# Layer 0 in three parts: the sample first, tile 0's mixer beside its gathers, then tile 1

## The reference, cut to what matters

```python
for l in range(2):
    h = rmsnorm(x, norm_mix[l])
    out = mixer_ab(h, ...) if l == 0 else mixer_c(h, k_past, v_past, ...)
    x = x + out
    x = x + peer(rmsnorm(x, norm_ffn[l]), w_query[l], sub_keys[l], u[l], v[l])

def peer(x, ...):                                # 8 heads, 128 x 128 keys, 16 experts each
    qry = (x @ w_query).reshape(t, 8, 2, 128)
    sc = einsum('thpd,pnd->thpn', qry, sub_keys)
    idx, top = top 16 of all sums s1[i] + s2[j], from the top 16 of each half
    act = gelu(einsum('thed,td->the', u[idx], x))
    return einsum('the,thed->td', softmax(top) * act, v[idx])
```

## Time and profile before

| | |
|---|---|
| median of 3 runs | 1945.54 us (1941.55 to 1947.11) |
| the profiled execution | 1943.43 us, span 1941.7 us |
| busy: TensorE, VectorE, ScalarE, GpSimd | 62%, 63%, 37%, 37% of the span |
| moved by DMA | 720.74 MB, mean 371 GB/s |
| gathers (queue of GpSimd) | 604.02 MB; all else by SyncE 113.84 MB |
| mean granted clock of TensorE | 0.738 of full speed |

### The profile page before, as it was taken

One profiled execution on the slowest core, in us unless ns is written; L12 is line 12 of the kernel. 1 busy time (PEld: TensorE's weight loads), 2 busy tenths in 40 slices (PEclk: granted clock), 3 DMA queues, 4 the chain that ended last, 5 costly groups with the idle time before them and its releaser, 6 DMA issues.

```text
span 1941.7 us, 25073 instructions
## 1 busy us (share of the span) xinstructions
PE 1212.1 (62%) x9288; PEld 739.9 (38%) x9288; DVE 1225.5 (63%) x3079; ACT 723.0 (37%) x1937; POOL 726.5 (37%) x651
## 2 busy tenths in 40 slices
PE   7998865566667539855579546665666644444443
PEld 7896742233335307733248224443325400000000
DVE  4541558888755575476654674557865667677664
ACT  2322145534432335274333333237533334333322
POOL 2021024545433433333133444434533444454442
PEclk9999875676788859966689658778679955555555
DMA  5645389999999999999599999999999999999996
GB/s 192 205 142 162 126 319 397 421 388 421 420 418 418 419 421 393 417 418 393 205 373 416 420 421 417 418 419 414 375 420 418 420 421 422 422 420 422 421 421 273
DMA packets 115658, 720.74 MB, mean 371 GB/s; under 512 B 13424, under 2 KB 13552, under 8 KB 41296
## 3 DMA queue, kind: packets, MB, share of 16 engines
q0 software_dynamic: 82944, 604.02, 75.6%
q1 hardware_dynamic: 31584, 113.84, 15.9%
q10 hardware_dynamic: 1008, 1.29, 0.2%
HBM read 714.98 MB, written 4.12 MB: 370 GB/s over the span
## 4 chain that ended last, share of the span: by engine, by line
DMA 46%; PE 27%; DVE 15%; ACT 6%; issue 4%; POOL 2%; ACTq 0%; POOLq 0%; DVEq 0%; SPq 0%
DMA sb_AR<-in_uv,sb_idx 44%; PE PS L1429 10%; DVE sb_AR L1011 7%; PE PS L1674 5%; PE PS L1651 2%; PE PS L1571 2%; PE PS L1694 1%; POOL sb_AR L513 1%; DMA sb_W<-in_w 1%; ACT sb_DG L576 1%; DVE sb_AR L1063 1%; ACT sb_gl L573 1%; PE PS L1815 1%; ACT L573 1%; DMA sb_lq<-in_lq 1%
## 5 line engine op out<-in xcount | busy, mean ns | idle before, releaser
L513 POOL DMA_INDIRECT sb_AR<-in_uv,sb_idx x576 | 695.2, 1207 | 1042.1 <-PE PS L1674 910.4
L1011 DVE CUSTOM_DVE_ANT_0 sb_AR<-sb_AR 128x1024 f32<-128x1024 f32 x576 | 703.9, 1222 | 452.3 <-DMA sb_AR<-in_uv,sb_idx 447.6
L1674 PE MATMUL PS<-sb_AR,sb_DG 128*32 128x256 f32 x4608 | 509.7, 528 | 582.2 <-ACT sb_DG L576 559.6
L1674 PEld LDWEIGHTS PS<-sb_AR,sb_DG 128*32 128x32 f32 x4608 | 128.9, 129 | 893.7 <-ACT sb_DG L576 802.1
L573 ACT ACTIVATE sb_gl<-sb_dots 128x1 f32<-128x1 f32 x576 | 116.2, 202 | 875.5 <-DVE sb_dots L1011 874.2
L1429 PE MATMUL PS<-sb_hT,sb_W 128*128 128x160 f32 (+1 forms) x2304 | 345.8, 310 | 8.6 <-ACT sb_hT L547 3.3
L1429 PEld LDWEIGHTS PS<-sb_hT,sb_W 128*128 128x128 f32 x2304 | 322.8, 208 | 50.6 <-issue 24.8
L576 ACT ACTIVATE sb_DG<-sb_GR,sb_gl 128x32 f32<-128x32 f32 x576 | 185.1, 321 | 18.7
L573 ACT ACT_TABLE_LOAD x68 | 87.2, 1283 | 1.1
L558 ACT ACTIVATE sb_AR<-sb_Hn 32x1024 f32<-32x1024 f32 x72 | 75.8, 1053 | 1.5
L1651 PE MATMUL PS<-sb_W,sb_mixT 128*128 128x512 f32 x128 | 69.8, 672 | 6.0 <-DMA sb_W<-in_w 4.8
(11 more groups left out here) (357 smaller groups left out, 1193.3 us busy)
## 6 DMA issues: line engine op xcount, KB each, us to landing
sb_W<-in_w SPq DMA_DIRECT2D x192, 512.0 KB, 7.9
sb_AR<-in_uv,sb_idx POOLq DMA_INDIRECT x576, 16.6
sb_gB<-in_gains SPq DMA_DIRECT2D x7, 512.0 KB, 7.7
sb_mixT<-in_kc SPq DMA_DIRECT2D x2, 1024.0 KB, 8.9
sb_hT<-in_vc SPq DMA_DIRECT2D x2, 1024.0 KB, 18.5
out_o_k<-sb_AR SPq DMA_DIRECT2D x1, 1152.0 KB, 9.2
sb_X<-in_x SPq DMA_DIRECT2D x2, 512.0 KB, 7.5
out_o_v<-sb_AR SPq DMA_DIRECT2D x1, 1024.0 KB, 14.3
```

The costliest lines, as they stand in the source:

```text
L513: g.indirect_dma_start(UV[:, sl, :], None, T[f"uv{layer}"], bass.IndirectOffsetOnAxis(ap=idx[:, c:c + 1], axis=0)).then_inc(S(f"uv_in{sl}" ...
L1011: v.tensor_tensor_reduce(UV[:, sl, 0:D], UV[:, sl, 0:D], Hrep[:, u % 2, :], 1.0, 0.0, ALU.mult, ALU.add, dots[:, sl:sl + 1]).then_inc(S("d ...
L1674: r = mm(PS[32 * q:32 * q + 32, 6 + u % 2, 0:256], DG[:, sl, :], UV[:, sl, o:o + 256], start=(c == 0), stop=(c == 31), skip_group_check=True)
```

## The change

Layer 0 becomes three parts: the sample alone (`VS`, one chunk), tile 0 (`V0`), tile 1 (`V1`). The input blocks of the sample and tile 0 stay common: 16 of them (queries, keys, values and the RG-LRU's input) come first, the other eight (the gates z and gb) join tile 1's 24 as filling. The sample's mixer has an inverse of six stages (its four heads with 32 frames each are one chunk of 128). The sample then has its own output projection, norm, queries and pick; its steps begin, and tile 0's mixer, projection and queries are placed beside the sample's mixer and its steps, tile 1's parts after that. Output projection and query weights of layer 0 are therefore loaded three times: 216 blocks in all.

All engines' queues are now made by one function, `weave`: each part yields the due time of its next stage, counted in steps (times before the first step are written in microseconds and converted), and the part with the smallest due time goes on. The weight list is sorted by the same due times. The first eight steps use four gather slots, because the other four hold tile 0's mixer; step 8 waits for its end (`mix_d` 2). Banks 6 and 7 of PSUM hold the small products of the sample.

In layer 1, keys and values are loaded separately: the first keys before the layer's weights, the first values after the 24 input blocks, the second keys after the first scores, the second values after the first group's products. TensorE waits for values only ahead of the products that use them, and the second group's products are due seven steps after its scores.

The diff, cut to its core:

```diff
-B_OUT0, B_QKV, NBLK = 24, 48, 96
-STREAM = list(range(24)) + IN_B + 2 * list(range(B_OUT0, B_QKV)) + 2 * list(range(B_QKV, NBLK))
-TILES = ((0, 2), (1,), (2, 0), (1,))
+TILES = ((2,), (0,), (1,), (2, 0), (1,))
-SPAN = ((0, 160), (160, 128), (0, 160), (160, 128))
+SPAN = ((128, 32), (0, 128), (160, 128), (0, 160), (160, 128))
...
+M4 = 8
+def slot(m):
+    return m % 4 if m < M4 else (m - M4 + 4) % UVS
+def slot_before(m):
+    return (m - 4 if m >= 4 else None) if m < M4 else (None if m < M4 + 4 else m - UVS)
...
+INVS = (INV[0:6], INV, INV)
+T_S, T_STEP = 133.0, 2.8
+def early(mp, rows):
+    for kind, n, us, k in rows:
+        for j in range(n):
+            PLAN[mp, kind, j] = (us + k * j - T_S) / T_STEP
+early(0, (("in", 16, 15, 2.2), ("gate", 1, 57.5, 0), ("lru", 1, 61.5, 0), ("dec", 1, 63, 0), ("at", 1, 67, 0),
+          ("kv", 1, 70, 0), ("inv", 6, 73, 2.4), ("lsq", 1, 80, 0), ("w", 1, 88, 0), ("vn", 1, 90, 0), ("o", 1, 92, 0),
+          ("on", 1, 94, 0), ("mix", 1, 97, 0), ("out", 8, 99, 0.6), ("norm3", 1, 105, 0), ("tr3", 1, 110, 0),
+          ("q", 16, 111, 1.4), ("hrep", 1, 132.7, 0)))
+early(1, (("dec", 1, 65, 0), ("at", 1, 70, 0), ("kv", 1, 74, 0), ("inv", 10, 78, 3.6), ("vn", 1, 116, 0),
+          ("o", 1, 120, 0), ("on", 1, 123, 0), ("mix", 1, 126, 0), ("out", 8, 136, 2), ("norm3", 1, 153, 0),
+          ("tr3", 1, 159, 0), ("hrep", 1, 160, 0), ("q", 16, 161, 2.4)))
+for _n in range(32):
+    _us = 49.9 + 2.2 * _n if _n < 4 else 60.2 + 2.2 * (_n - 4) if _n < 8 else 72.5 + 3.6 * (_n - 8)
+    PLAN[2, "fill", _n] = (_us - T_S) / T_STEP
+PLAN[0, "pick", 0] = at(0, "q", 8) + 0.1
...
+put(2, at(2, "fill", 31) + 1, (("conv", 16, 0.8),))
+put(2, max(at(1, "q", 15), at(2, "conv", 15)) + 2,
+    (("sq", 1, 0), ("l2", 1, 3), ("qu", 8, 1.5), ("gate", 1, 2), ("lru", 1, 3), ("dec", 1, 3), ("at", 1, 4),
+     ("kv", 1, 4), ("inv", 10, 3), ("w", 1, 3), ("vn", 1, 2), ("o", 1, 2), ("on", 1, 3), ("mix", 1, 2), ("out", 8, 1.25),
+     ("norm3", 1, 0), ("tr3", 1, 3), ("q", 16, 2)))
+put(3, 163, (("begin", 1, 0), ("norm2", 1, 3), ("qkv", 24, 1.25), ("head", 10, 2), ("smp", 3, 3), ("pvs", 1, 7),
+             ("on", 1, 3), ("out", 8, 1), ("norm3", 1, 0), ("tr3", 1, 3), ("q", 16, 1.5)))
...
+FILL = [(0, j) for j in range(16, 24)] + [(1, j) for j in range(24)]
+USES = [((0, "in", j), IN_F[j]) for j in range(16)] + [((2, "fill", n), IN_F[FILL[n][1]]) for n in range(32)]
+for _mp in range(5):
+    if _mp > 2:
+        USES += [((_mp, "qkv", j), B_QKV1 + j) for j in range(24)]
+    USES += [((_mp, "out", j), (B_OUT0, B_OUT1)[_mp > 2] + j) for j in range(8)]
+    USES += [((_mp, "q", j), (B_Q0, B_Q1)[_mp > 2] + j) for j in range(16)]
+USES.sort(key=lambda u: PLAN[u[0]])
+STREAM = [b for _, b in USES]
+def weave(*streams):
+    heads = [[next(g), k, g] for k, g in enumerate(streams)]
+    while heads:
+        h = min(heads, key=lambda x: x[0:2])
+        t = next(h[2], None)
+        if t is None:
+            heads.remove(h)
+        else:
+            assert t >= h[0], (t, h[0])
+            h[0] = t
...
+            eng.wait_ge(S("blk"), POS[2, "out", 7] + 1)
+            cache_k(0)
+            upto(3, "qkv", 0)
...
+            upto(3, "out", 0)
+            cache_v(0)
+            eng.wait_ge(S("s_qks"), 1)
+            cache_k(1)
+            eng.wait_ge(S("pvs"), 1)
+            cache_v(1)
...
+            def steps():
+                t = -0.5
+                for m in range(NSTEP):
+                    b = slot_before(m)
+                    t = t if b is None else max(t, b + PE_LAG + 0.5)
+                    yield t
+                    grp, layer = m // 16, m // (32 * 9)
+                    if m % 16 == 0:
+                        eng.wait_ge(S("idx"), grp + 1)
+                    if m == 0:
+                        eng.wait_ge(S("x_mix"), 1)
+                    if m == M4:
+                        eng.wait_ge(S("mix_d"), 2)
+                    if b is not None:
+                        eng.wait_ge(S("vsum"), b + 1)
...
+            weave(lru(), mixer0(0), mixer0(1), steps())
...
+            weave(part0(), gates(0), part1(), fill(), early_hrep(), early_gates(), convs2(), rest(), gates(2), steps())
...
+            weave(part0(), part1(), lru0(), rest(), lru1(), early_picks(), steps())
...
                     eng.wait_ge(S("kc"), 16 * (gq + 1))
-                    eng.wait_ge(S("vc"), 16 * (gq + 1))
...
                     eng.wait_ge(S("pts"), gq + 1)
+                    eng.wait_ge(S("vc"), 16 * (gq + 1))
...
+            weave(part0(), gates(0), part1(), fill(), rest(), steps())
```

More of the change, by code:

```diff
@@ L55, in unit_of @@
     return (2, 0) if k == 0 else ((k - 1) // 4, (k - 1) % 4)
[L58 to L81, removed]
@@ new lines, in count, with inv_sem, inv_count, turn @@
+        def count(name, p, n):
+            return n + sum(RAISED[name][0:p])
+        def inv_sem(name, p):
+            return S(name if p else name + "_s")
+        def inv_count(name, has, p, st):
+            return count(name, p, sum(has[n] for n in INV[0:st + 1]))
+        def turn(u):
+            i = TURN.index(u)
+            return 4 + i % 2, TURN[i - 2] if i >= 2 else None
+        def q_bank(mp, j):
+            return turn((mp, "q", j))[0] if mp < 2 else 4 + j % 2
+        def tr_ps(k, t, half):
+            w = ROWS[t]
+            v = PS[:, 6 + half, 256:384] if k == 3 else PS[:, 2 * t + half, 0:4 * w]
+            return v.rearrange("p (a b) -> p a b", b=w)
@@ L504, in _ @@
[L504 to L514 removed]
+            g.tensor_copy(V1.PJ[:, :, 0:3], J.PJ[:, :, 128:131])
@@ new lines, in early_hrep, with early_gates, part0, part1 @@
+            def early_hrep():
+                yield at(1, "hrep")
+                for r in range(4):
+                    hrep(1, r)
+            def early_gates():
+                yield at(0, "gexp")
+                gate_exp(0)
+                for k in range(2):
+                    yield at(1, "gexp", k)
+                    gate_exp(2 + k)
+            def part0():
+                yield from front()
+                yield from mixer0(0)
+                yield from tail(0)
+            def part1():
+                yield from mixer0(1)
+                yield from tail(1)
@@ L1289, in residual, with part0, part1, rest @@
                     r.then_inc(S("x_mix"), 1)
-            mixer0(0, keep)
-            residual(0)
-            norm(2)
-            eng.wait_ge(S("ev0b"), 24)
-            eng.wait_ge(S("cso"), 1)
-            for f in range(16):
-                conv(1, f)
-            for part in range(16):
-                pick(0, part)
-            def pace(mp):
-                return lambda kind, j=0: run.upto(PLAN[mp, kind, j])
-            def part1(upto):
-                upto("sq")
+                norm(FFN_NORM[mp])
+                yield at(mp, "tr3")
+                evac_hT(FFN_NORM[mp])
+            def part0():
+                yield from front()
+                yield from mixer0(0)
+                yield from tail(0)
+            def part1():
+                yield from mixer0(1)
+                yield from tail(1)
+            def rest():
+                for f in range(16):
+                    yield at(2, "conv", f)
+                    eng.wait_ge(S("fill"), 32)
+                    eng.wait_ge(S("cso"), 1)
+                    conv(2, f)
+                yield at(2, "sq")
                 for k in range(2):
@@ L1485, in mixer0, with fill, gates @@
+            def fill():
+                for n, (own, j) in enumerate(FILL):
+                    u = (2, "fill", n)
+                    yield PLAN[u]
+                    if n == 0:
+                        eng.wait_ge(S("ba"), 1)
+                    turn_free(u)
+                    block_fm(POS[u], turn(u)[0], *((COL[1], 128) if own else (0, 160)))
+            def gates(p):
+                yield at(p, "gate")
+                M, cw = (J, None, V1)[p], (163, None, 128)[p]
                 eng.wait_ge(S("conv"), count("conv", p, 16))
+                if p == 0:
+                    eng.wait_ge(S("l2_sqrt"), 8)
```

1705 lines of the change are left out of this document (829 added, 876 removed).

## The result

The change makes the kernel slightly slower. The median of 20 executions is 1953.4 us, against 1944.3 us for 20 of the kernel before beside them; the ratio is 1.0046 [1.0031, 1.0061], and 1.0047 [1.0028, 1.0066] when both ran once more. The forecast was 1926 us and faster; its range, up to 1954, just holds the time.

The account below looks back on a forecast made before the run. Transfers were taken to bound the kernel, losing time only below 421 GB/s: 1741 us used plus 181 unused gave a span of 1922, forecast 1926 us and faster, range 1894 to 1954.

Parts of the forecast that it names:

- First gather: Layer 0's front: first gather at about 192 us, 59 earlier (bounds 172 and 215), 48 us of transfer time won.
- the sum of TensorE's queue: Work queued on TensorE ahead of and through the sample's ninth query block: 168 us, before stalls.
- the 14 charged for stalls: Microseconds added to TensorE's 168 us for queue stalls before the first gather, giving 182; the old queue had 21.
- the rival of the stalling chain: Sample's 17 hand-over stages stall all in-order queues, 60 us lost, first gather at 238: 1972 us; chance 0.13.
- From the first gather to step 32: Stretch after the first gather: 15 us of transfer time unused against 9.4, 6 us lost; bounds 5 and 35.
- they stay the bound: Between first gather and step 32, transfers (56 MB, 134 us) remain the limit, against 113 us of TensorE work.
- The rival of the eaten head start: Full TensorE slows transfers to 382 GB/s after the first gather, some 36 us unused: 1947 us; chance 0.15.
- Added bytes: 24 more layer-0 weight blocks, 12.6 MB, total 733.3 MB: 30 us more transfers at 421 GB/s.
- Tile 1's squeeze: Tile 1's mixer beside the gathers, squeezed from about 141 to 118 steps: 3 us lost, bounds 0 and 10.
- Past keys and values: Layer 1's attention over the cache: separate, earlier loads win 10 of 29.5 unused us; bounds 0 and 20.
- What would show it: Signs: 733 MB, first gather near 192 us, first dot product near 212, long stretches at 414 GB/s, no 10 us TensorE wait.
- the 105 us: Transfer time forecast to go unused before the first gather, instead of 153 us.

Follow-up runs that it names:

- the two by two: Changed kernel with tile 0's 24 added blocks loaded in part: 1.0015; its layer-0 query blocks at one of eight matmuls: 1.0050; both: 0.9941 (to the kernel before).

## Why the prediction was wrong

**First gather (192 us, 48 us won).** Here it failed most. The first gather came at 211, and 27 us were won. The step that failed is the sum of TensorE's queue, which took the query block at 1.9 us and filling blocks at 1.8, durations read where the clock was full, and so priced the whole queue at full clock. From 159.35 to 201.7 us stand nine query blocks with eight scores, three filling blocks and three groups of tile 0's products, some 27 us at those prices; they took 42: 15 of the 19 us by which the first gather was late. At full clock the price was right (1.91 us). The narrow blocks lowered the clock: made wide, or with more wide ones between them, they left it at 1.00 and 0.96. TensorE's waits from 62.7 to 176.4 us, 19 us, are near the 14 charged for stalls, so the rival of the stalling chain, with 60 us of them, did not come.

The trace of the kernel before held the sign. The products of 8 columns from which the 1.9 us was taken start at 29.10 us; with others of 8 columns behind them they last to 33.85. Before they end the clock falls to half, and it stays there until 39 us, with TensorE busy all the time:

```profile
28.00:32.00 4.00, 4.00 (x37) 4.00 (x35) 0.00 (x0) 1.28 (x1) 0.00 (x0) 1.00 0.79 242
33.00:39.00 6.00, 6.00 (x83) 5.98 (x78) 4.68 (x24) 0.66 (x4) 0.50 (x1) 0.50 0.01 1
```

The clock is not the whole miss. With wide query blocks the ratio is 0.9960, where the forecast, 1926 against 1945.54 us, was 0.990.

The Trainium skill ("TensorE: Matmul & The Clock Gate", section "HAM oscillation — how this bites in real kernels") puts the fall down to gaps in which the engine waits. Here the trace differs. A wait of 2.2 us ends at 157.28 us, shortly before the first fall, but no wait stands between 160 and 202 us, where the clock falls again by 171 and by 184 us; and with wide query blocks a wait of the same 2.2 us, ending at 162.23, was followed by 1.00. The measurement decides: gaps are not needed.

**From the first gather to step 32 (6 us lost).** 21.8 us went unused, 12 more than before, within the bounds of 5 and 35. Two steps were mis-sized. The first dot product came 27 us after the first gather (238), not 20, since it waits behind all of the last seven query blocks and what lies between them; with that wait moved, 7 us came back, though with wide query blocks no such gain is shown. And "they stay the bound" was half the truth: from 280 to 352 us TensorE's queue binds beside the transfers, as the two by two shows. The rival of the eaten head start, 1947 us, gave about the right time by luck. Its reason was wrong: from 280 to 352 us the transfers ran at 417 GB/s, not 382, and most of what went unused lies ahead of that, from 202 to 250 us (230 GB/s), where the fifth gather waits.

**Added bytes (30 us).** The bytes came as counted, and the sum with them adds up to the span (1742 + 202, where 1942 was measured). As a saving they are worth only 6 us (1 to 12) where tile 0's blocks lie, since TensorE has no room to use it.

**Tile 1's squeeze (3 us).** 7.6 were lost, within the bounds, nearly all between 352 and 550 us. Giving the stages more room did not bring it back in the profile; the cause stays open.

**Past keys and values (10 us).** Right in place and mechanism: 10 us fewer unused in that stretch by the profile of the loads alone, and 10 to 19 in time. In the changed kernel the stretch leaves 10.1 us, at the far bound of 20 won; there other work falls into it as well (VectorE is busy 80.96 us of it, with the loads alone 71.27).

**What would show it.** 733 MB, the stretch from 1000 us on (416 GB/s against 415) and the vanished TensorE wait came as listed. The first gather, the first dot product and the 105 us did not, and the other long stretch fell from 414 to 408. Of the three signs named as what would make the forecast wrong, long gaps on TensorE did not come (the longest between 65 and 182 us is 6.6 us). The other two did: the transfers ran below 380 GB/s from 215 to 340 us, and tile 1's squeezed mixer, from 352 to 550 us, fell to 395.

```profile
215.00:340.00 125.00, 102.02 (x734) 78.87 (x734) 68.37 (x189) 52.18 (x107) 27.29 (x25) 0.89 0.90 354
```

No sign was named for what cost most, a slow clock on a full queue.

## What to carry to other kernels

A price for a matmul block holds only at the clock at which its row was read: look at the granted clock behind the row, and in the new order, before trusting the sum, and beware of narrow matmuls in a row where TensorE sets the pace; computing unused columns cost nothing here and won 17 us. Work moved beside gathers is free only if every engine, not the transfers alone, has room there, and taking away one limit shows little while a second stands behind it. Time a small independent part of a large change by itself: here it held all of the gain that was measured.

## What the runs showed of the hardware

TensorE was busy without a pause from 160 to 202 us and was granted 0.62 of its clock, with query blocks of 32 columns; with the same weights and 128 columns it was granted 1.00, and the first three blocks took 5.52 us instead of 8.70. Within that stretch one block of 32 columns took 1.91 us at 2.4 GHz and another 3.62 us at 1.2 GHz.

With less work for TensorE from 280 to 352 us (44.69 us busy instead of 61.28), the mean granted clock there fell from 0.96 to 0.80, so the matmuls that were left there ran slower.
